# A hybrid decoder step on one core: attention's last stores on another queue, the output projection's loads reordered, a shorter table, and other orders in the experts' loops

## The reference

```python
h = rmsnorm(x, g_n1) * (1 + sc1) + sh1
q, k, v, u_val, u_gate = split(h @ w_in)
att  = combine_branches([banded_dilated_branch(q, k, v, rel_bias, w, d)
                         for w, d in ((128, 1), (512, 4), (2048, 16))])   # 8 heads of 64
conv = silu(layernorm(causal_dwconv(u_val * sigmoid(u_gate)), ln_g, ln_b))
x = x + gt1 * (concat([att, conv]) @ w_out)
h2 = rmsnorm(x, g_n2) * (1 + sc2) + sh2
# router: best of 4 groups, best 2 of its 8 experts; expert: (silu(h @ w1) * (h @ w3)) @ w2
x = x + gt2 * hierarchical_moe(h2, ...)     # 32 experts of 1024 x 512, 512 x 1024
y = rmsnorm(x, g_final)
```

## Time and profile before

| what | value |
|---|---|
| median of three runs | 2343.29 us |
| the profiled execution, its own time | 2340.75 us |
| its span in the profile | 2339.2 us |
| PE busy | 1981.8 us (85%) |
| DVE busy | 1610.3 us (69%) |
| ACT busy | 1073.1 us (46%) |
| POOL busy | 576.4 us (25%) |
| mean DMA rate | 237 GB/s |

### The profile page before, as it was taken

The page is one execution under the profiler, slowest core; times in us unless marked ns, Lnnn a source line. Parts: engine busy times, 40 slices in busy tenths (PEclk is TensorE's granted clock), DMA queues, the critical chain, the costliest instruction groups (busy, mean ns, idle before and its releaser), DMA issues. The chain is left out here.

```text
span 2339.2 us, 40473 instructions
## 1 busy us (share of the span) xinstructions
PE 1981.8 (85%) x13004; PEld 1598.6 (68%) x13005; DVE 1610.3 (69%) x3110; ACT 1073.1 (46%) x2055; POOL 576.4 (25%) x564
## 2 busy tenths in 40 slices
PE   5999999997999988439999749899999998999910
PEld 3788888886777766217888637788777876878700
DVE  2568888888566667628999648766455675548778
ACT  2311111112777778005444237665445564547533
POOL 1024444440111112202555321101100111010066
PEclk8999999999999999669999869999999998999955
DMA  8855555554646466774787449968575977679777
GB/s 264 271 194 198 198 196 198 181 187 140 224 133 205 132 223 233 237 239 155 241 274 265 139 166 347 364 243 305 190 273 199 344 276 282 250 250 377 289 294 292
DMA packets 221017, 553.66 MB, mean 237 GB/s; under 512 B 28477, under 2 KB 43413, under 8 KB 219768
## 3 DMA queue, kind: packets, MB, share of 16 engines
q1 hardware_dynamic: 176464, 435.12, 53.2%
q0 software_dynamic: 25440, 76.21, 9.0%
q10 hardware_dynamic: 19024, 41.18, 5.0%
HBM read 457.38 MB, written 167.63 MB: 267 GB/s over the span
## 5 line engine op out<-in xcount | busy, mean ns | idle before, releaser
L597 DVE SCALAR_TENSOR_TENSOR ARENA<-ARENA,TAPW 128x512 f32<-128x512 f32 (+3 forms) x493 | 293.3, 673 | 0.0
L2383 DVE TENSOR_TENSOR LO<-WIDE,HI 128x2048 fp32r<-128x2048 f32 x128 | 284.5, 2283 | 4.3 <-ACT HI L2302 4.3
L2302 ACT CAST HI<-WIDE 128x2048 fp32r<-128x2048 f32 x128 | 240.1, 1910 | 56.0 <-DMA WIDE<-in_w_expert_gate 37.2
L423 POOL TENSOR_TENSOR MS<-SSQ,K 128x1 f32<-128x1 f32 x17 | 170.4, 10021 | 291.6 <-ACT H L466 291.6
L2383 DVE TENSOR_TENSOR LO<-W2E,HI 128x2048 fp32r<-128x2048 f32 x64 | 143.7, 2285 | 92.3 <-ACT HI L2302 92.3
L716 PE MATMUL PJ<-WIN_H,HTH 128*128 128x512 f32 x680 | 173.9, 399 | 15.0 <-ACT HTH L472 11.7
L1027 ACT ACTIVATE PR<-SBX,NM 128x256 f32<-128x256 f32 (+1 forms) x384 | 171.9, 455 | 2.3 <-DVE NM L961 2.3
L720 PE MATMUL PJ<-WIN_H,HTL 128*128 128x512 f32 x680 | 168.4, 390 | 0.0
L724 PE MATMUL PJ<-WIN_L,HTH 128*128 128x512 f32 x680 | 168.0, 389 | 0.0
L498 ACT ACTIVATE ARENA<-PJ 128x512 f32<-128x512 f32 x51 | 30.4, 598 | 292.9 <-PE PJ L724 292.9
L716 PEld LDWEIGHTS PJ<-WIN_H,HTH 128*128 128x128 f32 x680 | 128.1, 191 | 46.4 <-ACT HTH L472 15.9
(11 more groups left out here) (338 smaller groups left out, 4348.0 us busy)
## 6 DMA issues: line engine op xcount, KB each, us to landing
WIDE<-in_w_expert_gate SPq DMA_DIRECT2D x64, 1024.0 KB, 6.6
WIDE<-in_w_expert_up SPq DMA_DIRECT2D x64, 1024.0 KB
W2E<-in_w_expert_down SPq DMA_DIRECT2D x64, 1024.0 KB
expert_rows<-YE ACTq DMA_DIRECT2D x40, 512.0 KB, 5.6
expert_rows<-NOROWS POOLq DMA_DIRECT2D x11, 1536.0 KB, 11.7
WAD<-in_w_ada SPq DMA_DIRECT2D x16, 1024.0 KB, 7.1
X<-in_x_prompt SPq DMA_DIRECT2D x31, 512.0 KB
QN<-q_rows SPq DMA_DIRECT2D x48, 256.0 KB, 3.0
```

The costliest lines, as they stand in the source:

```text
L423: pool.tensor_tensor(MS[:], SSQ[:], const("eps"), ALU.add).then_inc(ms_ready, 1)
L597: ins = nc.vector.scalar_tensor_tensor(out=out, in0=src, scalar=tap, in1=out, op0=ALU.mult, op1=ALU.add)
L2302: nc.scalar.copy(HI[n][:, cols], raw[n][:, cols]).then_inc(hi_ready[n], 1)
L2383: nc.vector.tensor_tensor(LO[n][:, cols], raw[n][:, cols], HI[n][:, cols], ALU.subtract).then_inc(lo_ready[n], 1)
```

## The change

Four parts of the kernel are edited.

1. Attention: the last step's stores (blocks 44 to 47) go from POOL's program to the end of SP's, with semaphores of their own, and SP waits for them at the end.
2. Output projection: the first conv tile CC and the layer norm's LN are loaded by ACT, LN on a semaphore of its own; gate, gain, shift and G2 by SP in round -1 after the second conv tile; WR and the bias by SP after the second tile's branches. DVE waits for the modulation in round 0 ahead of the second tile's moments, for LN in round -1, for the bias at the first logits; PE waits for WR at the first logits. In round -1 PE turns the first mix ahead of the second conv tile. "lower" isn't loaded.
3. Table: two copies and five additions of shifted tiles of 128 x 2 x 32 take the place of the two products and two reductions of 128 x 1024.
4. Experts: ACT and DVE take w3 of the first expert directly after its w1; POOL starts both first index loads at once and fetches a run's next small block behind that run's blocks, with its index load ahead of the wait for PE; PE waits for the next small rows at a small block's end and no longer in every block; DVE subtracts the first half of the next w1 ahead of GE, the rest where it was.

```diff
# prompt_attention
@@ sync
+                for q in range(4):
+                    g = Round(STEPS - 1, q, STEPS - 1)
+                    r = g.at - 8 * SEGMENT
+                    sp.wait_ge(nm_ready, g.count(0, 2, 2))
+                    sp.wait_ge(exp_done, g.count(0, 2, 2))
+                    sp.dma_start(dilated(dr["stat"][2], DILATIONS[2], r, 0, P), ML[q][:]).then_inc(last_ml_out, 16)
+                    sp.wait_ge(o_taken, g.count(0, 1, 1))
+                    sp.dma_start(dilated(dr["num"][2], DILATIONS[2], r, 0, P), O[q % 2][:]).then_inc(last_o_out[q % 2], 16)
+                sp.wait_ge(last_ml_out, 64)
+                for n in range(2):
+                    sp.wait_ge(last_o_out[n], 32)
@@ gpsimd
-                with pool.Fori(2 * SEGMENT, 3 * SEGMENT) as s:
+                with pool.Fori(2 * SEGMENT, 3 * SEGMENT - 1) as s:
# output_projection_and_routing
@@ sync, round_
+                    if isinstance(i, int) and i == -1:
+                        for dst, part in ((GATE, 2), (GAIN, 4), (SHIFT, 3)):
+                            sp.dma_start(dst[:, 0], dr["mod"][DEC:DEC + 1, ...].to_broadcast([P, D])).then_inc(mods_in, 16)
+                            sp.dma_start(dst[0:DEC, 1], dr["mod"][0:DEC, ...]).then_inc(mods_in, 16)
+                        sp.dma_start(G2[:], t["g_norm2"].to_broadcast([P, D])).then_inc(mods_in, 16)
                     if there(i - 1):
...
                         wait(sp, att_ready, taken)
                         load(i + 2, ahead)
+                    if isinstance(i, int) and i == -1:
+                        sp.dma_start(WR[:, :, 0:GROUPS], t["w_router_group"][0].rearrange("(k p) n -> p k n", p=P)).then_inc(weights_in, 16)
+                        sp.dma_start(WR[:, :, GROUPS:], t["w_router_expert"][0].rearrange("(k p) n -> p k n", p=P)).then_inc(weights_in, 16)
+                        sp.dma_start(BR[:, 0:GROUPS], t["b_router_group"].to_broadcast([P, GROUPS])).then_inc(bias_in, 16)
+                        sp.dma_start(BR[:, GROUPS:], t["b_router_expert"].to_broadcast([P, NEXP])).then_inc(bias_in, 16)
@@ sync, before the rounds
-                load_conv(0, 0)
                 load(0, 0)
                 for k in range(4):
                     sp.dma_start(WO[:, 2 * k:2 * k + 2], ...).then_inc(wo_in[k], 16)
-                sp.dma_start(WR[:, :, 0:GROUPS], ...).then_inc(weights_in, 16)
-                sp.dma_start(WR[:, :, GROUPS:], ...).then_inc(weights_in, 16)
-                sp.dma_start(state["lower"][:], t["constants"][:, at:at + width]).then_inc(lower_in, 16)
@@ scalar
-                for n, (dst, part) in enumerate(((GATE, 2), (GAIN, 4), (SHIFT, 3))):
-                    act.dma_start(dst[:, 0], ...).then_inc(mods_in, 16)
-                    act.dma_start(dst[0:DEC, 1], ...).then_inc(mods_in, 16)
-                act.dma_start(G2[:], t["g_norm2"].to_broadcast([P, D])).then_inc(mods_in, 16)
+                act.dma_start(CC[:], dr["conv"]...[:, :, 0:P]).then_inc(cc_in, 16)
-                    act.dma_start(LN[:, 0], ...).then_inc(mods_in, 16)
-                    act.dma_start(LN[:, 1], ...).then_inc(mods_in, 16)
-                act.dma_start(BR[:, 0:GROUPS], ...).then_inc(mods_in, 16)
-                act.dma_start(BR[:, GROUPS:], ...).then_inc(mods_in, 16)
+                    act.dma_start(LN[:, 0], ...).then_inc(ln_in, 16)
+                    act.dma_start(LN[:, 1], ...).then_inc(ln_in, 16)
@@ vector
-                dve.wait_ge(mods_in, 16 * 11)
-                stt(GAIN[:, 0], GAIN[:, 0], 1.0, G2[:], ALU.add, ALU.mult).then_inc(gain_ready, 1)
-                stt(GAIN[0:DEC, 1], GAIN[0:DEC, 1], 1.0, G2[0:DEC], ALU.add, ALU.mult).then_inc(gain_ready, 1)
-                nc.vector.tensor_scalar(LNH[:], LN[:], 0.5, None, ALU.mult).then_inc(lnh_ready, 1)
...
                     if there(i):
                         conv_rest(i)
+                    if isinstance(i, int) and i == 0:
+                        dve.wait_ge(mods_in, 16 * 7)
+                        stt(GAIN[:, 0], GAIN[:, 0], 1.0, G2[:], ALU.add, ALU.mult).then_inc(gain_ready, 1)
+                        stt(GAIN[0:DEC, 1], GAIN[0:DEC, 1], 1.0, G2[0:DEC], ALU.add, ALU.mult).then_inc(gain_ready, 1)
                     if there(i + 1, TILES - 1):
                         moments(i + 1)
@@ tensor, round_
-                            pe.wait_ge(weights_in, 32)
...
+                    if isinstance(i, int) and i == -1:
+                        turn_mix(0)
                     if there(i + 2, TILES - 1):
                         turn_conv(i + 2)
@@ experts_table
-                    below(RUN, SMALL1)
-                    below(FROM, FULL)
+                    then(nc.vector.tensor_copy(SUMS[0][:, 0, NEXP + 1:], SMALL1[:, 0:NEXP - 1]))
+                    then(nc.vector.tensor_copy(SUMS[0][:, 1, NEXP + 1:], FULL[:, 0:NEXP - 1]))
+                    for n in range(5):
+                        now, to = SUMS[n % 2], SUMS[1 - n % 2]
+                        then(nc.vector.tensor_tensor(to[:, :, NEXP:], now[:, :, NEXP:], now[:, :, NEXP - 2 ** n:2 * NEXP - 2 ** n], ALU.add))
# experts
@@ gpsimd
                 def fetch_small(e, n):
                     slot = place(e * CAP, T)
-                    pool.wait_ge(sx_turned, n)
+                    pool.wait_ge(sx_in, pool.snap(n * 16 - 16))
                     pool.dma_start(IDXS[:], dr["slot"][ds(slot, T), :]).then_inc(sidx_in, 16)
                     pool.wait_ge(sidx_in, n * 16)
+                    pool.wait_ge(sx_turned, n)
                     pool.indirect_dma_start(XGS[:], ...).then_inc(sx_in, 16)
...
-                with pool.Fori(0, pool.snap(runs(pool) + 1)) as g:
+                second = place(entry(pool, 0, 1, 1, LAST) * CAP, T)
                 pool.dma_start(IDX0[:], dr["slot"][0:T, :]).then_inc(first_idx_in, 16)
+                pool.dma_start(IDXS[:], dr["slot"][ds(second, T), :]).then_inc(sidx_in, 16)
                 pool.wait_ge(first_idx_in, 16)
                 pool.indirect_dma_start(XG0[:], ...).then_inc(first_x_in, 16)
+                pool.wait_ge(sidx_in, 16)
+                pool.indirect_dma_start(XGS[:], ...).then_inc(sx_in, 16)
+                with pool.Fori(0, runs(pool)) as g:
                     head, behind = run(pool, g)
-                    fetch_small(entry(pool, 5, g + 1, 0, LAST), g + 1)
                     with pool.Fori(head, behind) as e:
...
+                        fetch_expert(e)
+                    fetch_small(entry(pool, 5, g + 2, 0, LAST), pool.snap(g + 2))
+                fetch_expert(LAST)
@@ scalar, at the start
                 upper(0, 0)
+                upper(1, 0)
                 take_small(0)
-                small(0, 0, first_expert)
+                small(0, 0, lambda: take_x(0))
@@ vector
-                def block_(b, split):
+                def block_(b, following=None):
+                    if following is not None:
+                        lower(0, following, (0,))
                     dve.wait_ge(s_ready, b + 2)
                     dve.wait_ge(b_done, b + 2)
...
                     rest_x(b + 1)
-                    for n in range(2):
-                        split(n)
+                    if following is not None:
+                        lower(0, following, (1,))
+                        lower(1, following)
@@ tensor
                     on_groups(YPS, GTS, W2[:], KF).then_inc(sy_done, 1)
+                    if not static:
+                        pe.wait_ge(sx_ready, n + 2)
...
                     pe.wait_ge(x_in, b * 16 + 32)
-                    pe.wait_ge(sx_ready, n + 1)
                     turn_x(range(6))
```

More of the change, by code:

```diff
@@ L108, in constant_columns @@
             parts["ownhead"][r, r % HEADS * DH:(r % HEADS + 1) * DH] = 1.0
-    parts["lower"] = np.tile((np.arange(NEXP)[None, :] < np.arange(NEXP)[:, None]).reshape(1, -1), (P, 1))
     parts["zero"] = np.zeros((P, NEXP * CAP // P))
@@ L846, in prompt_attention @@
         o_out, ml_out = ([sem(f"{x}_out{n}") for n in range(slots)] for x, slots in (("o", 2), ("ml", 4)))
+        last_o_out, last_ml_out = [sem(f"last_o_out{n}") for n in range(2)], sem("last_ml_out")
         loading = sem("loading")
@@ L1003, in take_rows @@
                     act.wait_ge(o_turned, g.count(back, 1, 1))
-                    if g.fixed:
+                    if g.fixed and g.at - back >= BLOCKS - 2:
+                        act.wait_ge(last_o_out[n], 16)
+                    elif g.fixed:
                         wait(act, o_out[n], 16 * ((g.at - back) // 2))
@@ L1622, in _ @@
                 pool.memset(NOROWS[:], 0.0).then_inc(norows_set, 1)
+                for n in range(2):
+                    pool.memset(SUMS[n][:], 0.0).then_inc(preset, 1)
                 def normalise(i):
@@ L2088, in logits @@
                     pe.wait_ge(h2t_ready, i + 1)
+                    if isinstance(i, int) and i == 0:
+                        pe.wait_ge(weights_in, 32)
                     wait(pe, logits_taken, i)
@@ L2105, in round_ @@
```

(16 more changed lines are left out.)

70 lines of the change are left out of this document (34 added, 36 removed).

## The result

The changed kernel takes 2290.98 us (median of 4 runs, 2287.70 to 2294.33), the kernel before on the same chip 2343.28 (2342.41 to 2346.63): a ratio of 0.9774, with a 95% interval from 0.9757 to 0.9792. That is 52.3 us less, where I had forecast 28.5 less and a time between 2300 and 2328. The sign was right, the size and the range were wrong.

What follows compares the result with a forecast made beforehand. Stages run one behind the other, with three empty seams, and PE bounds the experts. Terms of -8.5 -15 -1 -2.5 -10 +9.5 -1 sum to -28.5 us, giving 2315 us; range 2300 to 2328.

Steps and rivals of the forecast that it cites:

- Attention's stores: End of attention: last stores on SP hide POOL's drain, next stage starts earlier; 8.5 us less, bounds 0.7 and 9.
- rival (b): End of attention: the drain isn't hidden and takes its 7.9 us where the stage ends; 2323 us, chance 0.10.
- Start of the projection: Output projection: 8.5 MB ahead of the second mix set an earlier first X; 15 us less, bounds 5 and 18.
- Rival (c): Projection's start is bound by bytes, WR's long issue blocks X and CC; 5 instead of 15, 2325 us, chance 0.12.
- Table: End of routing: 3.5 us less on DVE, but only POOL's copy shrinks; 1 us less, bounds 0 and 3.5.
- First expert: First expert's gathers: second index load's issue and wait leave POOL's chain; 2.5 us less, bounds 0 and 4.
- Two late gathers: Experts: index load ahead of POOL's wait ends two of PE's three XG waits; 10 us less, bounds 4 and 11.
- The third wait: Experts: PE's third wait for XG, put down to a gather on full DMA engines, was to stay.
- The early half of LO: Experts: DVE's half ahead of GE delays PE at eight run heads; 9.5 us more, bounds 0 and 14.
- The DMA-bound stretch: Experts, 1410 to 1502: earlier load of w1 gives back 1 of 3.1 us, bounds -3 and 5.
- (a): Experts: DVE has room for the early half, the 9.5 vanish and 4 more are won; 2301 us, chance 0.20.
- (d): Experts: DVE's early half becomes the block's pace, holding GE, G's transposes and YP; slower, 2376 us, chance 0.03.

Runs made afterwards that it cites:

- experiment 1: Kernel before with only attention's last stores moved from POOL to SP: 2338.35 us against 2343.73, ratio 0.9971.
- experiment 2: Kernel before with only the new start of the projection and the new table: 2325.89 us against 2343.73, ratio 0.9929.
- 9: Kernel before with only the new table (sums by shifts), one run: 2343.03 us against 2342.25.
- Experiment 4: Changed kernel with POOL's old order of gathers in the experts, DVE's new order kept: 2297.98 us, ratio 0.9816 to the kernel before.
- Experiment 6: Changed kernel with POOL gathering in the order PE asks, a run's first block ahead of the small block behind it: 2278.74 us, ratio 0.9720.
- Experiment 3: Changed kernel with both halves of LO of w1 behind XL again, as before: 2302.24 us, ratio 0.9826 to the kernel before.
- experiment 5: Changed kernel without the early half, second half of LO of w3 moved to the next expert's head: 2292.68 us, ratio 0.9780.
- 7: Changed kernel with the edits of experiment 5 and Experiment 6 together: 2279.42 us, ratio 0.9732 to the kernel before.
- 8: The kernel of 7 with the early half of LO of w1 at every expert but a run's first: 2276.81 us, ratio 0.9709.
- 11: The kernel of 8 measured again, beside a repeat of the changed kernel on the same chip: 2276.81 us, ratio 0.9730 to the kernel before.

## Why the prediction was right and wrong

**Attention's stores: right.** 8.5 forecast, 8.9 from the last copy to the next stage. The drain is hidden; rival (b), where it is not, falls with experiment 1. The last store landed 2.0 us behind its issue, and not 2.5. Against (b) I had said that a drain follows how much POOL issued just before; with its last store 6.7 us back POOL's still took 7.25.

**Start of the projection: right in size, in part by luck.** 15 forecast, 16.4 to the first X counted from the stage's start, and 16.0 at the stage's end with the table in it. The sum by bytes put the second mix 33.2 us behind the stage's start; it was done at 33.6. But the bytes were not what it waited for: the second tile's branches had landed at 1041.3, the DMA share from 1040 to 1044 was 0.57, and DVE worked with one wait of 0.3 us from LN's landing at 1029.0 to 1048.1 (eight parts of w_out, GAIN, the second tile's moments and mix, 19.1 us in all). DVE came to the branches 1.9 us behind their landing, so the sum by bytes came out near. The term for WR was too large: its two issues took 2.4 and 5.6 us, not 11.1, and the CC behind them kept PE waiting for 0.5 us. Rival (c) falls by experiment 2, which has this part and the same gain (first X 32.8 us behind the first load of w_out, 48.5 before): the bytes are nearly the same, but DVE's first work no longer stands behind all of them. That loads started by different engines share the DMA engines, as the Trainium skill has it (DMA: Bandwidth & Descriptors, Issuing engines are not separate DMA queues), agrees with what the engines moved: 322 GB/s at a share of 1.00 with SP's and ACT's loads under way before, 355 at 1.03 after, with all but three of them from SP. But from that I could not conclude that only issue time is to be won: the loads changed their place in time as well as their engine.

**Table: right in kind.** 0.6 us and not 1. POOL's copy of SLOT shrank by 1.0, from 1.17 to 0.19, but its last scatter took 1.65 and not 1.06. The copy was not the price, as experiment 1 shows (under 9); what the last scatter's length hangs on stays open. DVE's 3.3 us lie beside POOL's drain.

**First expert: too large.** 0.7 in the trace, and 1.1 between the means of four traces of the old kind and the two of the new, against 2.5. My bound of 0 held. Experiment 4 shows both sides: with the new order on ACT and DVE but the old gathers it takes 24.7 us, against 23.0 to 23.7 before, and the new gathers win 2.4 from there.

**Two late gathers: wrong.** 10 forecast, nothing found (31.8 and 32.3 with the old order, 31.6 and 31.9 with the new). The step that failed is "With the index load ahead of the wait, some 5.8 us leave the chain, more than either lateness". The load did leave the chain, 5.9 and 5.7 us, but the steps behind it took 4.1 and 5.4 us longer (from the gather of XGS to PE's XG 19.0 and 19.4 us, 15.0 and 14.0 before), so from the end of POOL's wait to XG only 1.9 and 0.4 us were won; why they take longer, no run separates. And the 5.8 us were taken against the old lateness, as if PE came at the same time: it now asks 3.8 and 2.2 us sooner behind the turn of the small block's rows, since GS is in time and the clock stays up. What PE was late for was XG, whose index and rows still stood behind the wait. Experiment 6 takes the wait itself out of the way and finds 12.8 us in the 34 intervals. The slower matmuls behind the late turns, 3 us in my sum, are 2.9 (27.9 and 27.1 against 26.05). "The third wait has another cause [...] and stays" was wrong too: it is gone after, and in experiments 3 and 4.

**The early half of LO: half of it left out.** The price was there, if too large: 9.5 forecast over eight heads, measured 0.9 to 1.2 at six of them, 5.9 us in all, and nothing at the two whose rows came late (in experiment 6, with the rows in time, all eight cost some 7). What I left out is the other end of the move: LO's four halves stood ahead of GS at each of nine small blocks, and with one less PE no longer waits for GS, 13.7 us in nine waits. "Within 0.6 of nothing elsewhere" is the step that failed: I followed the moved half to GE, which it now precedes, and not to GS, which it no longer delays. The nine intervals are 0.6 to 3.7 us shorter each, 19.8 in all, and together with the heads that makes -14.3 in the 34 intervals instead of -0.5. Nor is this the wait alone: of two intervals with a wait of 1.65 to 1.7 us for GS, the one at full clock took 27.5 and the one at a mean clock of 0.94 took 28.5, and PE's busy time fell by 12.1 us. My sum had no term for a clock that falls behind a wait in the small blocks. Experiment 3 shows the same the other way round, and experiment 5 gets GS in time by another order; where a small block lost its wait for GS and no gather was late, the clock stayed at 1.00 in every trace.

**The DMA-bound stretch: mis-sized.** 1 forecast, 8.2 in the trace, outside its bounds of -3 to 5. "Of these 3.1 us I take 1" was worked out from PE's busy time at a mean share; the stretch from 1410 to 1502 has only part of the six blocks, and in this stretch PE in full work is busy 107 of 109 us, not at the mean share. The failed term is that 1: PE's own waits there were 6.0 us for GH and 1.7 for the XG that I had staying, and both are gone. Experiments 3, 4 and 5 show the way: the load of w1 is issued 5.5 to 8.6 us sooner, and ACT no longer waits for it (16.3 us in ten waits). Without the early half ACT waits again (10.4 and 16.1 us in experiments 3 and 5) and PE for GH (2.6 and 5.5).

**The rivals.** (a), DVE has room, came nearest with 2301, but its reason is not what happened: the eight heads do pay. (d) did not come: PE waits for GE only at six heads, and once for 0.5 us in the DMA-bound blocks. In the terms of the sum: 28.5, and 13.8 more in the 34 intervals (the nine with a small block 19.8 less, where I had 10 for the gathers; the heads 5.9 more and not 9.5; 0.4 in the others), 7.2 in the DMA-bound blocks, 1.0 behind the last turn and 0.5 in attention, less 1.8 in the first expert and 2.7 in decode, make the 46.4 of the traces; 5.9 lie between the traces and the medians.

What stays open: the last 0.7 to 1.0 us behind the last turn of X, why the decode stage takes up to 5.5 us more in some executions, what share of the DMA-bound stretch is the first expert's new order, and why the steps behind XGS take longer in the changed kernel.

## What to carry to other kernels

When work is moved ahead on an in-order engine, follow it at both ends: what it now delays, and what it no longer delays, here an operation of another loop that was nine times late. The list of waits by releaser names both; a row of 13.7 us in nine waits on the bounding engine was to be seen before the change. Price such a wait with the clock behind it: of the 14.3 us that the 34 intervals won, 12.1 were PE's busy time, with the same matmuls at a higher granted clock. A load ahead of a wait left the gather behind that wait as late as it was; with the queue of gathers in the order in which PE asks for them, the wait cost nothing.

## What the runs showed of the hardware

POOL's drain at the end of attention took 7.90 us in the three traces with the old stores, where POOL's last one was issued 2.6 us ahead of it, and 7.25 in the ten with the new, where it was issued 6.7 us ahead; the waits for all landings stand ahead of it, so it does not just wait for the last store to land. At the end of routing it took 3.74 or 3.75 in every trace, at the end of the experts 11.7 to 12.7.

PE's granted clock fell to the 1.2 GHz level nine times in the 34 intervals of the kernel before, at waits of PE for GS or XG, twice in the changed kernel, and not at all in experiments 6, 7, 8 and 11. PE was busy 690.1, 677.9 and, in experiment 6, 674.9 us with the same matmuls.

A small copy on POOL took 1.17 or 1.18 us beside a 1024-column operation of DVE, and 0.18 to 0.19 beside short ones.

The decode stage, with the same instructions, took from 67.3 to 72.9 us. Projection and routing took 319.0 to 322.7 in the ten traces with its change, the six DMA-bound blocks 110.5 and 111.2 for one kernel, and attention's last copy ended anywhere from 936.0 to 941.4. In the first table those ends are 940.8 and 940.7, so its first row holds little of that spread. A block of the experts that waits for nothing repeats within 0.05 us.
